# The low parts of the split weights move from VectorE to GpSimd, in a four-layer fp32 transformer kernel

## The chip, the cores and the metric

The kernel runs on one core of a Trainium2 chip. The metric is the device time of one execution in microseconds (us); lower is better. The time before is the median of three runs.

## The reference, cut to what matters

Two different transformer blocks run one after the other on the same residual (512 latent tokens, width 1024, plus 256 context tokens in the first block), each with two layers, so four layers in all. Every layer is: a modulated norm, a wide input projection, mixers (linear attention, neighbourhood and window attention in the first block; sparse attention and an mLSTM in the second), an output projection, a second modulated norm, and a gated feed-forward part. The weights stay fp32.

```python
h = rms_norm(x, g1) * (1 + scale) + shift
p = h @ w_in                       # 2848 columns in layers 1, 2; 3408 in layers 3, 4
y = mixers(p) @ w_out
x = x + gate * y                   # y is normed first in layers 3, 4
h = rms_norm(x, g2) * (1 + scale) + shift
y = (silu(h @ w_gate) * (h @ w_up)) @ w_down    # 2816 hidden columns
x = x + gate * y                   # y is normed first in layers 3, 4
```

## The kernel before, in words

TensorE takes its operands as fp32r, a rounded form. To keep accuracy each big product is made as three: high x high, high x low, low x high, where `high` is the rounded value and `low` is the value minus `high`, rounded again. This holds for the weights and for the activations (`h_high`, `h_low`, `hidden_high`, `hidden_low`).

The weights of a layer come as 108 split slices ("units"), 432 in the whole kernel, of up to 1024 columns on 128 partitions. Within a layer the order is fixed: 32 slices of the input projection (712 columns in layers 1 and 2, 852 in layers 3 and 4), 8 of the output projection, then three parts (`PARTS`) of the feed-forward. The first part has 16 gate and up slices and 8 down slices, the second and the third 14 and 8. Seven does not divide by two, so in each of those two parts the last slice of each half of the down projection has only 512 columns and half the matmuls. All other slices of the output projection and of the feed-forward have 1024.

Each slice goes through a chain of engines:

1. SyncE loads it into one of four landing slots (`weights`). Slot j is loaded again when `w_low` says that the low part of slice j - 4 has been made.
2. ScalarE makes the high part (`split()` of the scalar block, line 869): it waits for the load and for TensorE to be done with slice s - 2, since `weights_high` and `weights_low` are double buffers.
3. VectorE makes the low part (`split()` of the vector block, line 1197), waits for `w_high`, and increments `w_low`.
4. TensorE waits for `w_low` and uses the slice (line 461 in `product`, line 788 for gate and up).

Every engine works through its own queue in order, and the place of a `split()` in it is written out by hand. VectorE's stand: two before each `modulate` and before the `low` loop of the output projection, so behind what VectorE did last (a norm, the end of the mixers) and ahead of what TensorE waits for next; one for each slice beside the input projection; and in the feed-forward before and between the products of gate and up, and ahead of `outputs`, which empties the banks of the down projection. `modulate` (lines 1219 and 1209) reads a turned bank, scales it into `scratch` and subtracts `h_high` to give `h_low`; TensorE needs `h_low` for its first slices and for reusing the banks.

GpSimd does next to nothing before: two memsets in each of layers 1 and 2 (lines 839 and 841).

Of the kernel before, what the change touches and what calls it, by code (L numbers as in the profile page):

```python
# [22 lines left out]
F32 = mybir.dt.float32  # L23
F32R = mybir.dt.float32r
I32 = mybir.dt.int32
ALU = mybir.AluOpType
# [41 lines left out]
LAND = 4  # L68
# [94 lines left out]
def layer(nc, T, w, sems, second, with_ctx, nxt, start_loads=()):  # L163
# [5 lines left out]
    S = sems  # L169
# [29 lines left out]
    slots = [WR[:, UNIT * i:UNIT * (i + 1)] for i in range(LAND)]  # L199
    WH, WL = ([T[n][:, UNIT * i:UNIT * (i + 1)] for i in range(2)] for n in ("weights_high", "weights_low"))  # L200
# [30 lines left out]
    weight_units = []  # L231
    split_of = []
# [126 lines left out]
    if not second:  # L359
# [6 lines left out]
        ZT = SC[0:33, 12288:13056]  # L366
        WZ = SC[0:33, 13056:13568]
# [51 lines left out]
    with nc.Block() as block:  # L419
# [414 lines left out]

        @block.gpsimd
        def _(pool):
            if not second:
                pool.wait_ge(S["h_ready"], 1)
                pool.memset(WZ, 0.0).then_inc(S["zeroed"], 1)
                pool.wait_ge(S["zeroed"], 1)  # L840
                pool.memset(ZT[32:33, :], 1.0).then_inc(S["z_ones"], 1)

        @block.scalar
        def _(act):
# [301 lines left out]
        def _(dve):  # L1146
# [9 lines left out]
            def copy_out(bank, dst):  # L1156
                dve.tensor_copy(dst, bank).then_inc(S["emptied_dve"], 1)
# [28 lines left out]
                for i, t in list(enumerate(tt))[::2]:  # L1186
                    dve.tensor_scalar(XNV[:, t, :], XV[:, t, :], rstd[:, i:i + 1], None, ALU.mult).then_inc(S["normed%d" % which], 1)

            nsplit, nhigh = [0], [0]

            def split():

                s_ = nsplit[0]
                nsplit[0] += 1
                _, _, (k, n), _ = weight_units[split_of[s_]]
                dve.wait_ge(S["w_high"], s_ + 1)
                dve.tensor_tensor(WL[s_ % 2][:, 0:k * n], slots[split_of[s_] % LAND][:, 0:k * n],  # L1197
                                  WH[s_ % 2][:, 0:k * n].bitcast(F32), ALU.subtract).then_inc(S["w_low"], 1)

            def after_high():  # L1200

# [165 lines left out]
            dve.sem_inc(S["scales"], 1)  # L1367
            if start_loads:
                norm(0, IN_T)
            split()  # L1370
            split()
            modulate(0, IN_T)
            dve.wait_ge(S["emptied_dve"], B.emptied_by("d"))
            dve.sem_inc(S["h_ready"], 1)
# [46 lines left out]

            for j in range(8):
                for i in range(4 if j < 7 else 3):
                    if (j, i) != (0, 0):
                        split()
                    if second:
                        beside_projection(j, i)
                for i, t in enumerate(IN_T):
                    bank = B.empty(dve, turn[i % 2], "d")
                    if bank is not None:  # L1430
                        copy_out(bank[:, 0:CW], pr(t, CW * j, CW))

            if not second:
# [36 lines left out]
                for k in range(NCH - 1):  # L1470
                    for d in range(2):
                        c, after = order[d][k], order[d][k + 1]
                        i = c // 2
# [9 lines left out]
                for n, t in enumerate(OUT_T):  # L1483
# [17 lines left out]
                    if t >= CTX_T:  # L1501
                        i = t - CTX_T
# [11 lines left out]
                n = 0  # L1514
# [99 lines left out]
                dve.sem_inc(S["mixed"], 1)  # L1614


            split()
            split()
            for f in range(KD):
                for a, cnt, r in spans(OUT_T):  # L1620
                    low(f, a, cnt, after_high()[:, 0:cnt])
# [33 lines left out]
                        copy_out(bank[:, :], y)  # L1655

            for j in range(2):
                for _ in range(3):
                    split()
                outputs(0, j)  # L1660
            if second:
                add_normed(0)
            norm(1, OUT_T)
            dve.sem_inc(S["mod_room"], 1)
            split()
            split()
            modulate(1, OUT_T)


            def ahead():  # L1670
                if nsplit[0] < len(split_of):
                    split()

            q = 0
            for m0, m1 in PARTS:
                for m in range(m0, m1):
                    if m:
                        ahead()
                    for _ in spans(OUT_T):
                        B.empty(dve, "a", "d")  # L1680
                    gated = B.emptied_by("a") - len(spans(OUT_T))
                    ahead()
                    for a, cnt, r in spans(OUT_T):
                        dve.wait_ge(S["emptied_dve"], B.emptied_by("d"))
                        bank = B.empty(dve, "d", "d")
# [7 lines left out]
                    if nxt:  # L1693
                        mod_tile(m)
                for half in range(2):
                    for k in range(m0, m1, 2):
                        ahead()
                    outputs(1, half, more=m0 > 0)
                    if nxt and m1 == KF:
                        mod_tile(KF + half)  # L1700
# [167 lines left out]
```

## Time and profile before

| | |
|---|---|
| runs | 4343.82 us median (4338.45, 4343.82, 4361.6) |
| span of the profiled execution | 4364.2 us; its own time is not listed among the three runs |
| busy: TensorE, VectorE, ScalarE, GpSimd | 3728.4, 2047.7, 1124.4, 2.7 us |
| mean granted TensorE clock | 0.884 |
| low parts on VectorE | 432 instructions, 486.8 us |

The profile page lists, for one execution, each engine's busy time and what it waited for. The timeline lists instructions in order of time: start, length, engine, line of the kernel, operation, what it writes and reads, how many were merged, and in square brackets how long the engine sat idle before it and what it waited for. The window view gives busy time by engine in a stretch. Durations below come from this one execution, so a sum made of them belongs beside its span.

### The profile page before, as it was taken

What the parts mean: (1) busy time and instruction counts of PE and PEld (TensorE: products, weight loads), DVE (VectorE), ACT (ScalarE), POOL (GpSimd) and SP (SyncE); (2) the same over time, 40 slices, a digit from 0 to 9 for tenths busy, and PEclk for the clock granted to TensorE, in tenths of its full rate; (3) what the DMA queues carried; (4) which work ended last, traced back from release to release, by engine and by line L of the source; (5) the groups of instructions that cost most, each with busy time, mean ns of one, the idle gap of its engine ahead of it and who ended that gap; (6) DMA issues with size and microseconds to landing.
All of it is one profiled execution on the core that took longest, in us unless ns stands there. A gap on an engine that the chain in (4) does not pass through costs nothing. (4 is left out here: it accounts for less than half of the span.)

```text
span 4364.2 us, 51771 instructions
## 1 busy us (share of the span) xinstructions
PE 3728.4 (85%) x21178; PEld 3105.1 (71%) x21178; DVE 2047.7 (47%) x3763; ACT 1124.4 (26%) x1884; POOL 2.7 (0%) x8
## 2 busy tenths in 40 slices
PE   4896899899998995998999693878999793678997
PEld 3895667688887995777878682546888691456886
DVE  0324566423333325664443538664333448765333
ACT  0312344311111212443222321233222322323222
POOL 0000000000000000000000000000000000000000
PEclk9996699899999995899999895559999896769999
DMA  8110000232332210003445320003454230002332
GB/s 294 49 52 1 25 1 30 58 122 91 107 102 84 56 46 3 22 18 109 151 135 158 92 85 0 0 10 91 141 169 150 84 89 10 1 17 75 97 97 73
DMA packets 315485, 326.95 MB, mean 75 GB/s; under 512 B 11082, under 2 KB 231794, under 8 KB 315122
## 3 DMA queue, kind: packets, MB, share of 16 engines
q1 hardware_dynamic: 315250, 323.64, 24.4%
q8 instruction: 169, 2.77, 0.3%
q14 instruction: 66, 0.54, 0.0%
HBM read 321.50 MB, written 2.10 MB: 74 GB/s over the span
## 5 line engine op out<-in xcount | busy, mean ns | idle before, releaser
L1197 DVE TENSOR_TENSOR weights_low<-weights,weights_high 128x1024 fp32r<-128x1024 f32 (+3 forms) x432 | 486.8, 1129 | 1278.8 <-ACT weights_high L869 1276.9
L869 ACT ACTIVATE weights_high<-weights 128x1024 fp32r<-128x1024 f32 (+3 forms) x432 | 423.8, 983 | 1407.3 <-PE bank L461 997.4
L788 PE MATMUL bank<-h_high,weights_high 128*128 128x512 f32 (+1 forms) x1760 | 658.5, 374 | 10.4 <-DVE h_low L1209 9.1
L788 PE MATMUL bank<-h_low,weights_high 128*128 128x512 f32 (+1 forms) x1760 | 649.9, 369 | 0.0
L788 PE MATMUL bank<-h_high,weights_low 128*128 128x512 f32 (+1 forms) x1760 | 648.8, 369 | 0.0
L461 PE MATMUL bank<-weights_high,h_high 128*128 128x356 f32 (+2 forms) x1568 | 546.0, 348 | 6.4 <-DVE h_low L1209 6.0
L461 PE MATMUL bank<-weights_low,h_high 128*128 128x356 f32 (+2 forms) x1568 | 545.1, 348 | 0.0
L461 PE MATMUL bank<-weights_high,h_low 128*128 128x356 f32 (+2 forms) x1568 | 543.6, 347 | 0.0
L788 PEld LDWEIGHTS bank<-h_high,weights_high 128*128 128x128 f32 x1760 | 332.9, 189 | 83.5 <-DVE h_low L1209 16.5
L788 PEld LDWEIGHTS bank<-h_high,weights_low 128*128 128x128 f32 x1760 | 333.0, 189 | 55.8
L788 PEld LDWEIGHTS bank<-h_low,weights_high 128*128 128x128 f32 x1760 | 333.3, 189 | 52.2
L461 PEld LDWEIGHTS bank<-weights_high,h_high 128*128 128x128 f32 x1568 | 296.0, 189 | 22.4 <-issue 7.1
L461 PE MATMUL bank<-weights_high,hidden_high 128*128 128x512 f32 x792 | 309.9, 391 | 1.5 <-DVE weights_low L1197 1.4
L461 PE MATMUL bank<-weights_low,hidden_high 128*128 128x512 f32 x792 | 308.3, 389 | 0.0
L461 PEld LDWEIGHTS bank<-weights_high,h_low 128*128 128x128 f32 x1568 | 297.9, 190 | 14.4
L461 PE MATMUL bank<-weights_high,hidden_low 128*128 128x512 f32 x792 | 308.1, 389 | 0.0
L461 PEld LDWEIGHTS bank<-weights_low,h_high 128*128 128x128 f32 x1568 | 296.8, 189 | 13.5
L570 PEld LDWEIGHTS bank<-constants,scratch 128*128 128x128 f32 x792 | 100.0, 160 | 223.8 <-ACT scratch L935 125.0
L583 PE MATMUL bank<-projected,scratch 128*128 128x128 f32 x1584 | 253.7, 311 | 0.1
L583 PEld LDWEIGHTS bank<-projected,scratch 128*128 128x128 f32 x1584 | 236.6, 227 | 1.4 <-issue 1.0
L570 PE MATMUL bank<-constants,scratch 128*128 128x128 f32 x792 | 156.6, 324 | 89.1 <-ACT scratch L935 57.9
L557 PE MATMUL bank<-scratch 64*128 64x512 f32 (+3 forms) x320 | 165.6, 607 | 51.0 <-ACT scratch L1063 51.0
(232 smaller groups left out, 4165.3 us busy)
## 6 DMA issues: line engine op xcount, KB each, us to landing
projected<-in_w_mod SPq DMA_DIRECT2D x96, 1024.0 KB, 5.2
weights<-in_w_gate_up SPq DMA_DIRECT2D x88, 512.0 KB, 4.0
weights<-in_w_down SPq DMA_DIRECT2D x80, 512.0 KB, 3.9
weights<-in_w_in SPq DMA_DIRECT2D x64, 426.0 KB, 3.4
weights<-in_w_in SPq DMA_DIRECT2D x64, 356.0 KB, 3.1
weights<-in_w_gate SPq DMA_DIRECT2D x44, 512.0 KB, 6.6
weights<-in_w_up SPq DMA_DIRECT2D x44, 512.0 KB, 7.7
weights<-in_w_out SPq DMA_DIRECT2D x32, 512.0 KB, 3.6
```

Of the source, the lines that this page charges most:

```text
L461: mm = pe.matmul(out_banks[t][:, 0:n], x[:, kk - off[0], at], wt[:, kk - k, :], start=(kk == k0 and q == 0), stop=(kk == k1 - 1 and q == 2))
L557: mm = pe.matmul(b[:, 0:u["nb"]], u["q"], u["kb"], start=True, stop=True)
L570: mm = pe.transpose(PS[4 + j // 4][:, (j % 4) * PT:(j % 4 + 1) * PT], src[:, j * PT:(j + 1) * PT], ident)
L583: mm = pe.matmul(PS[6 + i % 2][:, 0:128], pb[:, j * PT:(j + 1) * PT], pr(t, c - u.get("off", 0), 128), start=(j == 0), stop=(j == len(u["v ...
L788: mm = pe.matmul(bank[:, 0:cnt], wt[:, k, :], x[:, k, a:a + cnt], start=(k == 0 and q == 0), stop=(k == KD - 1 and q == 2))
L869: act.activation(WH[s_ % 2][:, 0:k * n], slots[j % LAND][:, 0:k * n], ACT.Copy).then_inc(S["w_high"], 1)
L1197: dve.tensor_tensor(WL[s_ % 2][:, 0:k * n], slots[split_of[s_] % LAND][:, 0:k * n], WH[s_ % 2][:, 0:k * n].bitcast(F32), ALU.subtract).the ...
```

## The change: what it does

The 432 subtractions go to GpSimd's queue. Their operands, their number and the semaphores `w_high` and `w_low` are the same. All of VectorE's `split()` calls go. In layers 1 and 2 GpSimd's two memsets, which wait for VectorE's `h_ready`, stand before the third low part.

```diff
         @block.gpsimd
         def _(pool):
-            if not second:
-                pool.wait_ge(S["h_ready"], 1)
-                pool.memset(WZ, 0.0).then_inc(S["zeroed"], 1)
-                pool.wait_ge(S["zeroed"], 1)
-                pool.memset(ZT[32:33, :], 1.0).then_inc(S["z_ones"], 1)
+            for s_, j in enumerate(split_of):
+                _, _, (k, n), _ = weight_units[j]
+                if not second and s_ == 2:
+                    pool.wait_ge(S["h_ready"], 1)
+                    pool.memset(WZ, 0.0).then_inc(S["zeroed"], 1)
+                    pool.wait_ge(S["zeroed"], 1)
+                    pool.memset(ZT[32:33, :], 1.0).then_inc(S["z_ones"], 1)
+                    pool.wait_ge(S["z_ones"], 1)
+                pool.wait_ge(S["w_high"], s_ + 1)
+                pool.tensor_tensor(WL[s_ % 2][:, 0:k * n], slots[j % LAND][:, 0:k * n],
+                                   WH[s_ % 2][:, 0:k * n].bitcast(F32), ALU.subtract).then_inc(S["w_low"], 1)
...
-            def split():
-
-                s_ = nsplit[0]
-                nsplit[0] += 1
-                _, _, (k, n), _ = weight_units[split_of[s_]]
-                dve.wait_ge(S["w_high"], s_ + 1)
-                dve.tensor_tensor(WL[s_ % 2][:, 0:k * n], slots[split_of[s_] % LAND][:, 0:k * n],
-                                  WH[s_ % 2][:, 0:k * n].bitcast(F32), ALU.subtract).then_inc(S["w_low"], 1)
...
                 norm(0, IN_T)
-            split()
-            split()
             modulate(0, IN_T)
...
             for j in range(2):
-                for _ in range(3):
-                    split()
                 outputs(0, j)
...
             dve.sem_inc(S["mod_room"], 1)
-            split()
-            split()
             modulate(1, OUT_T)
...
                 for half in range(2):
-                    for k in range(m0, m1, 2):
-                        ahead()
                     outputs(1, half, more=m0 > 0)
```

The other calls of `split()` and `ahead()` in the vector block (beside the input projection, before the `low` loop of the output projection, and around the products of gate and up) go in the same way.

## Rows read from the trace of the kernel before

**Rows 1.** The page, part 1: busy us, share of the span, instructions.
```profile
PE 3728.4 (85%) x21178; PEld 3105.1 (71%) x21178; DVE 2047.7 (47%) x3763; ACT 1124.4 (26%) x1884; POOL 2.7 (0%) x8
```

**Rows 2.** Windows: length, busy us of each engine (instructions), clock, DMA share, GB/s.
```profile
811.00:1390.00 579.00, 575.99 (x3626) 490.70 (x3627) 199.75 (x295) 90.06 (x114) 0.00 (x0) 0.99 0.32 99
...
3978.00:4342.00 364.00, 360.94 (x1587) 296.61 (x1585) 143.24 (x168) 84.08 (x95) 0.00 (x0) 1.00 0.29 87
```

**Rows 3.** Groups of VectorE instructions by shape: busy us, mean ns, idle before.
```profile
L1197 DVE TENSOR_TENSOR weights_low<-weights,weights_high 128x1024 fp32r<-128x1024 f32 x288 | 351.4, 1222 | 830.0 <-ACT weights_high L869 829.0
...
L1691 DVE TENSOR_TENSOR hidden_low<-projected,hidden_high 128x512 fp32r<-128x512 f32 x88 | 60.9, 692 | 3.0
...
L1197 DVE TENSOR_TENSOR weights_low<-weights,weights_high 128x712 fp32r<-128x712 f32 x64 | 57.5, 901 | 233.1 <-ACT weights_high L869 232.9
```

**Rows 4.** Waits of TensorE: us in total, times, longest us.
```profile
PE bank L461 <- DVE weights_low L1197: 1.9, 3, 1.2
```

**Rows 5.** Timeline, feed-forward of layer 4, ScalarE and VectorE.
```profile
4031.56 1.05 ACT L869 ACTIVATE weights_high<-weights 128x1024 fp32r<-128x1024 f32 x1
...
4036.56 1.06 ACT L869 ACTIVATE weights_high<-weights 128x1024 fp32r<-128x1024 f32 x1 [3.95 <-PE bank L788]
...
4032.64 1.23 DVE L1197 TENSOR_TENSOR weights_low<-weights,weights_high 128x1024 fp32r<-128x1024 f32 x1 [3.82 <-ACT weights_high L869]
```

**Rows 6.** Timeline, input projection of layer 3, VectorE and ScalarE.
```profile
2517.70 1.05 DVE L1197 TENSOR_TENSOR weights_low<-weights,weights_high 128x852 fp32r<-128x852 f32 x1 [3.62 <-ACT weights_high L869]
...
2521.42 0.92 ACT L869 ACTIVATE weights_high<-weights 128x852 fp32r<-128x852 f32 x1 [0.70 <-PE bank L461]
```

**Rows 7.** Timeline, down projection of layer 2, around a slice of 512 columns.
```profile
2252.17 1.06 ACT L869 ACTIVATE weights_high<-weights 128x1024 fp32r<-128x1024 f32 x1 [4.81 <-PE bank L461]
...
2253.26 1.23 DVE L1197 TENSOR_TENSOR weights_low<-weights,weights_high 128x1024 fp32r<-128x1024 f32 x1 [5.18 <-ACT weights_high L869]
...
2254.55 0.19 PEld L461 LDWEIGHTS bank<-weights_high,hidden_high 128*128 128x128 f32 x1 [0.17 <-DVE weights_low L1197]
...
2260.20 2.50 DVE L1197 TENSOR_TENSOR weights_low<-weights,weights_high 128x1024 fp32r<-128x1024 f32 x2
...
2261.48 0.50 PE L461 MATMUL bank<-weights_high,hidden_high 128*128 128x512 f32 x1 [1.19 <-DVE weights_low L1197]
```

**Rows 8.** Timeline of GpSimd.
```profile
148.50 0.52 POOL L839 MEMSET scratch<- 33x512 f32 x1 [148.05 <-DVEq L1374]
149.08 0.73 POOL L841 MEMSET scratch<- 1x768 f32 x1
```

**Rows 9.** Timeline, end of the mixers of layer 3.
```profile
2929.92 1.99 ACT L869 ACTIVATE weights_high<-weights 128x1024 fp32r<-128x1024 f32 x2
...
2930.33 2.29 DVE L1239 TENSOR_TENSOR projected<-projected,small 128x2048 f32<-128x2048 f32 x1
...
2934.98 2.29 DVE L1243 TENSOR_TENSOR projected<-projected 128x2048 f32<-128x2048 f32 x1
2937.41 5.84 PEld L759 LDWEIGHTS bank<-constants,projected 128*128 128x128 f32 x32 [13.26 <-issue]
```

**Rows 10.** Timeline, second norm of layer 3, VectorE and ScalarE.
```profile
2989.71 1.28 DVE L1639 SCALAR_TENSOR_TENSOR projected<-projected,small,gates 128x1024 f32<-128x1024 f32 x1
...
3005.91 0.81 DVE L1219 TENSOR_SCALAR scratch<-bank,small 128x512 f32<-128x512 f32 x1 [0.56 <-PE bank L480]
...
2989.37 1.99 ACT L869 ACTIVATE weights_high<-weights 128x1024 fp32r<-128x1024 f32 x2
```

**Rows 11.** Timeline, first modulation of layer 1.
```profile
127.77 1.71 DVE L1197 TENSOR_TENSOR weights_low<-weights,weights_high 128x712 fp32r<-128x712 f32 x2 [1.81 <-ACT weights_high L869]
...
129.97 0.42 DVE L1209 TENSOR_TENSOR h_low<-scratch,h_high 128x256 fp32r<-128x256 f32 x1
```

**Rows 12.** Timeline, start of the output projection of layer 1.
```profile
714.06 2.36 DVE L1197 TENSOR_TENSOR weights_low<-weights,weights_high 128x1024 fp32r<-128x1024 f32 x2
...
714.52 6.97 ACT L1094 ACTIVATE h_high<-bank 128x256 fp32r<-128x256 f32 x16 [1.89 <-PE bank L759]
...
716.34 5.99 DVE L1209 TENSOR_TENSOR h_low<-bank,h_high 128x256 fp32r<-128x256 f32 x13
```

More of the change, by code:

```diff
@@ L1187, in norm @@
                     dve.tensor_scalar(XNV[:, t, :], XV[:, t, :], rstd[:, i:i + 1], None, ALU.mult).then_inc(S["normed%d" % which], 1)
-            nsplit, nhigh = [0], [0]
-            def split():
-                s_ = nsplit[0]
-                nsplit[0] += 1
-                _, _, (k, n), _ = weight_units[split_of[s_]]
-                dve.wait_ge(S["w_high"], s_ + 1)
-                dve.tensor_tensor(WL[s_ % 2][:, 0:k * n], slots[split_of[s_] % LAND][:, 0:k * n],
-                                  WH[s_ % 2][:, 0:k * n].bitcast(F32), ALU.subtract).then_inc(S["w_low"], 1)
+            nhigh = [0]
             def after_high():
@@ L1423, in _ @@
                 for i in range(4 if j < 7 else 3):
-                    if (j, i) != (0, 0):
-                        split()
                     if second:
@@ L1657, in _ @@
             for j in range(2):
-                for _ in range(3):
-                    split()
                 outputs(0, j)
@@ L1664, in _ @@
             dve.sem_inc(S["mod_room"], 1)
-            split()
-            split()
             modulate(1, OUT_T)
-            def ahead():
-                if nsplit[0] < len(split_of):
-                    split()
             q = 0
@@ L1676, in _ @@
                 for m in range(m0, m1):
-                    if m:
-                        ahead()
                     for _ in spans(OUT_T):
@@ L1681, in _ @@
                     gated = B.emptied_by("a") - len(spans(OUT_T))
-                    ahead()
                     for a, cnt, r in spans(OUT_T):
@@ L1695, in _ @@
                 for half in range(2):
-                    for k in range(m0, m1, 2):
-                        ahead()
                     outputs(1, half, more=m0 > 0)
```

## The prediction

> **What bounds the kernel now.** I read the page first: TensorE is busy for 85% of the span and VectorE for 47% [rows 1], so nothing that merely relieves VectorE pays on average. The window view then splits the span. In the stretches of weight products TensorE is busy without a break: 575.99 of 579 us in the first feed-forward, 360.94 of 364 in the last [rows 2]; thirteen such windows hold 2868 us, with TensorE busy for 2822. Only the list of waits says what the low parts cost there, and it is almost nothing: 1.9 us in 3 waits [rows 4], one more of 1.2 us on the feed-forward line, and 13.3 us of weight loads held back, mostly the same places. The rest of the time lies between products, in norms, mixers and modulations, where VectorE and TensorE take turns. So the change can act in three places: in the chain of a slice beside the products, at the slices with no slack, and where a low part stands in or beside a VectorE chain on which TensorE waits.
>
> **What one low part costs on GpSimd.** The trace before has no such instruction. On VectorE 1024 columns take 1222 ns [rows 3], and that is the lower end. GpSimd's only rows are memsets: 512 columns in 0.52 us and 768 in 0.73 [rows 8], so 0.82 ns for each column written, and some 0.1 us besides. If the two reads pass in turn, 1024 columns take 0.1 + 2 x 0.84 = 1.8 us; if the write takes its turn too, 0.1 + 3 x 0.84 = 2.6. I take the middle, 2.2 us, 1.0 more than VectorE; 1.85 for 852 columns, 1.55 for 712, 1.2 for 512. All 432 come to some 870 us, a fifth of the span, so GpSimd is not full.
>
> The Trainium skill, GPSIMD Engine Reference, section 3.1, gives 4497 ns for a two-input fp32 instruction of 2048 columns; half of that, as an estimate, is 2.25 us, and the sum would be the same.
>
> **Beside the products: nothing.** In layer 4, ScalarE's high part starts at 4031.56, VectorE's low part ends at 4033.87, and TensorE closes the slice before at 4036.56, when the next high part starts [rows 5]. TensorE runs on about 0.2 us before that, so 2.4 us are spare, and 1.0 is used. In the input projection of layers 3 and 4 the low part ends at 2518.75 and the next high part starts at 2521.42 [rows 6]: again 2.4 spare, of which 0.8 is used. Layers 1 and 2 have 3.8 there. I went through all 432 slices in this way, comparing the end of the low part with the first matmul of its slice. Half the gate and up slices have less, 2.04, but there the low part stood 0.86 to 1.06 us behind VectorE's own work, which GpSimd doesn't do, so they lose next to nothing. SyncE's loads wait for `w_low` too and start 1 us later, but three slices (over 14 us) ahead of use. The two memsets, 1.3 us with their waits, now delay the third low part of layers 1 and 2, with 3.8 us spare. What covers all this is the 4.7 us and more that TensorE needs for a slice; the cover ends at a low part of about 3.6 us.
>
> **Slices after a short one: +6.9.** A slice of 512 columns keeps TensorE only 2.9 us in layers 2 to 4. The next slice's high part runs 2252.17 to 2253.23, its low part to 2254.49, and TensorE loads it at 2254.55 [rows 7]: 0.14 us spare by the matmuls. There are seven such places (two in layers 2 and 3, three in layer 4), and one in layer 2 where the load was late (0.06 spare). 8 x (1.0 - 0.14) = +6.9 us.
>
> **Where VectorE's queue held the low part back: -3.0.** In layer 2 two slices waited 4.25 us for VectorE, busy emptying banks, and TensorE stalled 1.19 us [rows 7], then 1.20, and 0.22 at a third; layer 3 has one of 0.44. GpSimd has no such queue: -3.0.
>
> **Output projection, layers 1 and 2: -2.6.** VectorE makes two low parts from 714.06 and reaches `h_low` at 716.34, while ScalarE has the first `h_high` by about 714.95 [rows 12]. Here the subtraction reads a bank, and TensorE's turning waits for emptied banks. It starts 1.3 us earlier, twice. In layers 3 and 4 the turning takes TensorE 5.84 us without waiting [rows 9], so there is nothing to gain. At the second modulation VectorE waits for a bank anyway (0.56 us, [rows 10]): also nothing.
>
> **VectorE chains that share time with GpSimd's new work: the term that decides.** The rows say which instructions will overlap, not whether they delay each other. If they can't run together, the second waits for all of the first, and only instructions with both inputs in SBUF count.
> - End of the mixers, layers 3 and 4. The high parts are ready at about 2930.95 and 2931.91, in the midst of three dependent VectorE instructions of 2.29 us from 2930.33 to 2937.27, after which TensorE, idle for 13.26 us, starts [rows 9]. VectorE waits on a semaphore between them, so GpSimd's low parts slip in: 2 x 2.2 = 4.4, in two layers +8.8.
> - Second norm, layers 3 and 4. The high parts come at about 2990.4 and 2991.36, and VectorE has eight dependent instructions from 2989.71 [rows 10]: again +4.4 in each, +8.8.
> - First modulation. In layers 1 and 2 two low parts would hold GpSimd until 127.8 + 3.1 = 130.9; `h_low` started at 129.97 [rows 11]: +0.9 each. In layers 3 and 4 from 2440.8 to 2444.5, against 2443.54: +1.0 each. Together +3.8.
>
> These are +21.4 if they exclude each other, and if not about -2 (the modulations start up to 0.5 us earlier). Which end? Rows before can't say, since GpSimd never ran beside VectorE. I take the upper end, because each low part needs the same reads that VectorE's instruction does and gives them back only when it ends.
>
> The Trainium skill, SBUF — State Buffer, section on the single rule, says that a VectorE instruction with two SBUF inputs contends with a GpSimd instruction that reads SBUF, and that the second to issue blocks until the first is done. No row here shows it. By that rule the sum is what I forecast; without it the sum is that of the first rival.
>
> **Sum.** +6.9 - 3.0 - 2.6 + 21.4 = +22.7 us on the profiled span of 4364.2, which makes 4386.9, or 0.52%. The span is 20 us above the median of the runs, and I add the same microseconds to the median: 4343.8 + 22.7 = 4366.
>
> **The rivals.**
> - No exclusion: GpSimd and VectorE run side by side. Sum +6.9 - 3.0 - 2.6 - 2 = -0.7: 4343 us, not slower. For it: the two engines have queues of their own, and nothing in the rows ties them. Against it: only the two-input argument. It decides by the lengths of the three 2.29 us instructions: unchanged, it holds.
> - GpSimd becomes the bound. If a low part takes over 3.6 us, every second gate and up slice stalls. At 4.5 us (twice my price): 4.5 - 1.22 - 2.4 = 0.9 us on about 130 slices of layers 2 to 4, plus 8 x 3.1 and four chains of two low parts, 9 each: +180, about 4520. Against it: it is far above the 2.6 us that three streams give.
> - The relief is worth more: VectorE's queue gets 487 us free. If all twelve stage starts moved by the two low parts that stood there (2.36 us at 1024 columns), -25 in all, with +6.9 for the short slices and -3.0: 4322. Against it: VectorE was idle at two kinds of start after them [rows 10], and TensorE turned without waiting [rows 9].
>
> **How the numbers follow.** Chances: exclusion (full or in part) 0.70, no exclusion 0.17, GpSimd as the bound 0.08, larger relief 0.05. The prediction is the first, 4366. With prices from 1.8 to 2.6 its sum runs from about +15 to +32, and with only some low parts landing in the chains it falls to about +5: its own range is 4349 to 4378. The range of 8 in 10 takes in the no-exclusion rival and some drift of the median (the three runs spread over 23 us): 4338 to 4388. A difference of 0.5% (21.7 us) is about what a measurement tells from none. The exclusion case ends above it about half the time: 0.36, and the bound case adds 0.08, so slower 0.44; faster 0.05; within it 0.51.
>
> **What would show it.** Right: low parts of about 2.2 us on GpSimd; the three instructions at the end of the mixers stretching from 6.9 to about 11.4 us in layers 3 and 4; TensorE waits for GpSimd of some 0.9 us after the short slices; the product windows otherwise unchanged; the 1.19 us stall gone. Wrong: two-input instructions of VectorE at their old lengths beside GpSimd (first rival), or TensorE waits for `weights_low` all along the feed-forward (second). The prediction fails most easily on the order at each boundary: if VectorE keeps its turn, both chains stay whole.

## The result and the profile after

| | before | after |
|---|---|---|
| median of 20 runs each, same chip | 4358.60 us (4325.03 to 4373.29) | 4390.73 us (4361.19 to 4416.52) |
| ratio, 95% interval | | 1.0078 (1.0056 to 1.0101) |
| span of the profiled execution | 4364.2 us | 4388.9 us |
| its mean granted TensorE clock | 0.884 | 0.874 |

The change makes the kernel slower, by 0.8%. The prediction was 4366 us, with 8 chances in 10 for 4338 to 4388; the median lies 2.7 us above that range. Two later timings of the same kernel, six runs each, gave 1.0100 (1.0059 to 1.0142) and 1.0103 (1.0062 to 1.0143).

The page after, part 1, answers to [rows 1]:

```profile
PE 3727.8 (85%) x21178; PEld 3105.0 (71%) x21178; DVE 1844.9 (42%) x3331; ACT 1124.0 (26%) x1884; POOL 968.2 (22%) x440
```

VectorE lost 486.8 us of work, but its busy time fell by only 202.8. The missing 284 us are the first sign: VectorE's other instructions became longer. The groups of instructions by shape say which (busy us, mean ns, idle before):

```profile
L846 POOL TENSOR_TENSOR weights_low<-weights,weights_high 128x1024 fp32r<-128x1024 f32 x288 | 704.4, 2447 | 2642.2 <-ACT weights_high L875 2642.2
L846 POOL TENSOR_TENSOR weights_low<-weights,weights_high 128x852 fp32r<-128x852 f32 x64 | 130.5, 2040 | 258.0 <-ACT weights_high L875 258.0
...
L1671 DVE TENSOR_TENSOR hidden_low<-projected,hidden_high 128x512 fp32r<-128x512 f32 x88 | 232.9, 2646 | 3.0
L1620 DVE TENSOR_TENSOR x_res<-x_res,projected 128x512 f32<-128x512 f32 x80 | 97.1, 1214 | 2.7
L1669 DVE TENSOR_TENSOR projected<-projected,bank 128x512 f32<-128x512 f32 x88 | 60.6, 688 | 596.7 <-PE bank L788 596.7
L1670 DVE TENSOR_TENSOR hidden_high<-projected,bank 128x512 fp32r<-128x512 f32 x88 | 59.8, 680 | 0.0
```

`hidden_low`, with both inputs in SBUF, took 692 ns before [rows 3] and takes 2646. Its two neighbours, which read a bank, stay at 0.69 us. A low part costs GpSimd 2.40 us when nothing disturbs it (2.45 on average), against 1.22 on VectorE [rows 3].

The timeline shows how the two engines exclude each other. First in the feed-forward of layer 4, which answers to [rows 5]:

```profile
4058.31 0.68 DVE L1670 TENSOR_TENSOR hidden_high<-projected,bank 128x512 fp32r<-128x512 f32 x1
4059.02 2.77 DVE L1671 TENSOR_TENSOR hidden_low<-projected,hidden_high 128x512 fp32r<-128x512 f32 x1
...
4058.85 2.40 POOL L846 TENSOR_TENSOR weights_low<-weights,weights_high 128x1024 fp32r<-128x1024 f32 x1 [2.62 <-ACT weights_high L875]
```

GpSimd reads from 4058.85 to 4061.25. `hidden_low` is issued at 4059.02 and ends at 4061.79, 0.54 us after GpSimd: it did nothing until GpSimd was done, and the profile counts its wait as busy time. It costs nothing, since VectorE's next instruction, at 4068.59, waits 6.79 us for TensorE anyway.

Then the down projection of layer 2, after a slice of 512 columns, which answers to [rows 7]:

```profile
2249.56 0.69 DVE L1618 TENSOR_TENSOR projected<-bank,gates 128x512 f32<-128x512 f32 x1 [16.75 <-PE bank L461]
2250.29 2.65 DVE L1620 TENSOR_TENSOR x_res<-x_res,projected 128x512 f32<-128x512 f32 x1
2252.97 0.69 DVE L1618 TENSOR_TENSOR projected<-bank,gates 128x512 f32<-128x512 f32 x1
2253.69 2.05 DVE L1620 TENSOR_TENSOR x_res<-x_res,projected 128x512 f32<-128x512 f32 x1
...
2250.01 2.37 POOL L846 TENSOR_TENSOR weights_low<-weights,weights_high 128x1024 fp32r<-128x1024 f32 x1 [4.58 <-ACT weights_high L875]
2252.73 2.47 POOL L846 TENSOR_TENSOR weights_low<-weights,weights_high 128x1024 fp32r<-128x1024 f32 x1 [0.34 <-ACT weights_high L875]
...
2252.44 0.50 PE L461 MATMUL bank<-weights_high,hidden_high 128*128 128x512 f32 x1 [0.94 <-POOL weights_low L846]
```

At 2252.97 an instruction that reads a bank and one SBUF operand runs wholly beside GpSimd (2252.73 to 2255.20) in its 0.69 us; the next, with two SBUF operands, ends at 2255.74, again 0.54 us after GpSimd. TensorE waits 0.94 us for the low part: the short slice. Its list of waits for GpSimd, which answers to [rows 4], has nine entries. Seven are the short slices; the other two, 0.64 and 0.80 us in layer 2, follow slices whose load was late (ScalarE had waited 2.88 and 3.05 us for it):

```profile
PE bank L461 <- POOL weights_low L846: 4.4, 5, 1.0
...
PE bank L788 <- POOL weights_low L846: 3.7, 4, 1.0
```

The windows of the first and the last feed-forward answer to [rows 2]:

```profile
813.10:1392.10 579.00, 575.23 (x3628) 490.50 (x3628) 183.84 (x230) 89.03 (x113) 156.24 (x66) 0.99 0.33 99
4003.00:4367.00 364.00, 358.38 (x1572) 294.57 (x1572) 107.41 (x97) 81.15 (x93) 154.04 (x66) 1.00 0.29 87
```

In the first window TensorE is as busy as before (575.23 of 579, 575.99 before), though GpSimd now has 156 us of low parts there. In the last it loses 2.6 us, most of it at three short slices.

The start of the output projection of layer 1 answers to [rows 12]:

```profile
713.95 4.67 POOL L846 TENSOR_TENSOR weights_low<-weights,weights_high 128x1024 fp32r<-128x1024 f32 x2 [393.01 <-ACT weights_high L875]
...
716.71 3.61 ACT L1100 ACTIVATE h_high<-bank 128x256 fp32r<-128x256 f32 x9 [1.89 <-PE bank L759]
717.20 0.42 DVE L1206 TENSOR_TENSOR h_low<-bank,h_high 128x256 fp32r<-128x256 f32 x1 [1.09 <-PE bank L759]
```

The first `h_low` now starts 0.49 us after the first `h_high`, not 1.82, and beside GpSimd's low part (to 718.62) it keeps its 0.42 us, as it reads a bank.

The end of the mixers of layer 3 answers to [rows 9]:

```profile
2925.71 2.29 DVE L1236 TENSOR_TENSOR projected<-projected,small 128x2048 f32<-128x2048 f32 x1
2926.41 8.13 POOL L846 TENSOR_TENSOR weights_low<-weights,weights_high 128x1024 fp32r<-128x1024 f32 x2 [338.92 <-ACT weights_high L875]
2928.03 4.31 DVE L1237 TENSOR_TENSOR projected<-projected 128x2048 f32<-128x2048 f32 x1
...
2932.38 4.31 DVE L1240 TENSOR_TENSOR projected<-projected 128x2048 f32<-128x2048 f32 x1
2936.82 5.45 PEld L759 LDWEIGHTS bank<-constants,projected 128*128 128x128 f32 x32 [17.29 <-issue]
```

The engines alternate at the boundaries between instructions. GpSimd is issued at 2926.41 but waits for VectorE's first instruction, which ends at 2928.00; then each of the next two VectorE instructions is 2.02 us longer, as it waits for a low part. The three take 10.98 us instead of 6.94 [rows 9], and TensorE is idle for 17.29 us instead of 13.26.

The second norm of layer 3 answers to [rows 10]:

```profile
2989.50 5.99 POOL L846 TENSOR_TENSOR weights_low<-weights,weights_high 128x1024 fp32r<-128x1024 f32 x2 [10.70 <-ACT weights_high L875]
2990.04 3.25 DVE L1631 TENSOR_TENSOR x_res<-x_res,projected 128x1024 f32<-128x1024 f32 x1
2993.21 3.36 DVE L1630 SCALAR_TENSOR_TENSOR projected<-projected,small,gates 128x1024 f32<-128x1024 f32 x1
...
2997.75 1.28 DVE L1630 SCALAR_TENSOR_TENSOR projected<-projected,small,gates 128x1024 f32<-128x1024 f32 x1
```

Two of VectorE's eight instructions grow, by 2.02 and 2.08 us. The first modulation of layer 1 answers to [rows 11]:

```profile
129.49 3.36 POOL L846 TENSOR_TENSOR weights_low<-weights,weights_high 128x712 fp32r<-128x712 f32 x2 [129.04 <-ACT weights_high L875]
...
131.65 1.48 DVE L1206 TENSOR_TENSOR h_low<-scratch,h_high 128x256 fp32r<-128x256 f32 x1
```

The first `h_low` ends at 133.13, 0.28 us after GpSimd.

The Trainium skill, SBUF — State Buffer, section Who interferes with whom, says that a VectorE instruction with two SBUF inputs contends with a GpSimd instruction that reads SBUF, and that the one that issues second blocks until the first is done. The trace agrees: the waiting instruction ends 0.54 us after GpSimd's in the feed-forward of layer 4 and in the down projection of layer 2, though it was issued 2.23 us before GpSimd's end at one place and 1.51 at the other.

### Where the microseconds went

I cut both executions at the same matmuls by their number, and took the difference of each stretch, from the first matmul on. Outside the mixers the change adds 23.2 us:

| term of the prediction | forecast | measured |
|---|---|---|
| slices after a short one, with VectorE's queue | +6.9 - 3.0 = +3.9 | +5.1 (layers 1 to 4: -0.15, +0.90, +1.42, +2.92) |
| start of the output projection, up to the first product | -2.6 | -3.0 (-1.01, -0.21, -0.39, -1.38) |
| first modulations | +3.8 | +4.2 (+1.05, +1.03, +1.08, +1.08) |
| end of the mixers, layers 3 and 4 | +8.8 | +7.9 (+4.03, +3.89) |
| second norm and turning, layers 3 and 4 | +8.8 | +10.0 (+5.25, +4.74) |
| all else outside the mixers (+2.3 of it ahead of the first modulation, where no low part had been made) | 0 | -1.0 |
| sum | +22.7 | +23.2 |

Two rows agree better than their reasons do. The forecast of the output projection was -1.3 us in each of layers 1 and 2 and nothing in layers 3 and 4. Layer 1 gave -1.0; in layer 2 the turning ran without a stop before and after (3.68 and 3.69 us), and only 0.2 was gained. The other -1.8 came from layers 3 and 4, where the 32 matmuls of the turning took 5.66 and 5.20 us at a granted clock of 0.64 and 0.70, against 6.05 and 6.58 at 0.60 and 0.55. The kernel before, run again, shows -0.6 and -0.3 at the same two places, and the kernel with nothing but two delays in each of layers 3 and 4 (below) -0.1 and -1.4. So over half of that row is luck. The second norm is taken up at the end.

The mixers themselves differ by +2.1 us in all, made of terms as large as -4.5 and +9.3, and there is not one low part inside them. The windows of the mixers of layers 3 and 4 show what goes with their length (length; busy us of TensorE, its weight loads, VectorE, ScalarE, GpSimd; granted clock; DMA share; GB/s). Before:

```profile
2596.73:2924.02 327.29, 210.87 (x683) 136.96 (x684) 221.02 (x555) 81.44 (x174) 0.00 (x0) 0.58 0.01 4
3594.81:3892.33 297.52, 175.59 (x684) 112.98 (x684) 219.89 (x555) 81.42 (x174) 0.00 (x0) 0.68 0.01 4
```

After:

```profile
2594.45:2919.41 324.96, 207.64 (x684) 134.03 (x684) 220.72 (x555) 81.41 (x174) 0.00 (x0) 0.60 0.01 4
3600.16:3906.94 306.78, 186.36 (x684) 120.54 (x684) 220.32 (x555) 81.41 (x174) 0.00 (x0) 0.66 0.01 4
```

The same 684 matmuls keep TensorE busy for 176 us at a granted clock of 0.68 and for 211 at 0.58. VectorE's work is the same in all four rows to 1.2 us. Keep this in mind for the experiments.

### The profile page after: what moved, and what is told of

Read it like the earlier page. It is cut to its first block and busy times, and to the rows that moved or that the text cites. A ratio compares the mean times of both kernels' runs of the same rounds, so it can differ in the third digit from the quotient of the medians.

```text
span 4388.9 us, 51755 instructions
## 1 busy us (share of the span) xinstructions
PE 3727.8 (85%) x21178; PEld 3105.0 (71%) x21178; DVE 1844.9 (42%) x3331; ACT 1124.0 (26%) x1884; POOL 968.2 (22%) x440
## 5 line engine op out<-in xcount | busy, mean ns | idle before, releaser
L846 POOL TENSOR_TENSOR weights_low<-weights,weights_high 128x1024 fp32r<-128x1024 f32 (+3 forms) x432 | 965.5, 2236 | 3354.6 <-ACT weights_high L875 3354.5
L1669 DVE TENSOR_TENSOR projected<-projected,bank 128x512 f32<-128x512 f32 (+1 forms) x110 | 69.8, 635 | 775.8 <-PE bank L788 775.8
L1163 DVE COPY projected<-bank 128x356 f32<-128x356 f32 (+2 forms) x112 | 66.7, 596 | 667.4 <-PE bank L461 667.4
L1671 DVE TENSOR_TENSOR hidden_low<-projected,hidden_high 128x512 fp32r<-128x512 f32 (+1 forms) x110 | 245.6, 2233 | 3.8
```

The costliest lines, as they stand in the source:

```text
L846: pool.tensor_tensor(WL[s_ % 2][:, 0:k * n], slots[j % LAND][:, 0:k * n], WH[s_ % 2][:, 0:k * n].bitcast(F32), ALU.subtract).then_inc(S["w ...
L1669: dve.tensor_tensor(FT[:, 0:cnt], SG[q % 2][:, 0:cnt], bank[:, 0:cnt], ALU.mult)
L1671: dve.tensor_tensor(GL[:, m - m0, at], FT[:, 0:cnt], GH[:, m - m0, at].bitcast(F32), ALU.subtract).then_inc(S["emptied_dve"], 1)
```

## The experiments

All times are compared with runs of the kernel before on the same chip. "Outside the mixers" is the difference of the stretches from the profiled execution of before, summed as above; I call it the profile sum, and it needs no timing. Most kernels share this edit, with another `on_vector` in each; VectorE's `split()` calls are back, and skip what GpSimd makes:

```diff
+def on_vector(second, s_):        # second: layers 3 and 4; s_: number of the slice
+    return s_ in (...)
...
+                if on_vector(second, s_):
+                    continue
+                if s_ and on_vector(second, s_ - 1):
+                    pool.wait_ge(S["w_low"], s_)
                 pool.wait_ge(S["w_high"], s_ + 1)
                 pool.tensor_tensor(...)
```

**Theory and rival.** Theory: the engines exclude each other, and three kinds of place pay for it (the first modulations, the end of the mixers, the second norm); the short slices pay for GpSimd's longer instruction. Rival: the time comes from anything GpSimd does all along (its load, its queue, TensorE's clock), and the places are only part of it.

### GpSimd waits until the chains are done

```diff
+                if second and s_ == 32:
+                    pool.wait_ge(S["mixed"], 1)
+                if second and s_ == 40:
+                    pool.wait_ge(S["mod_room"], 1)
```

> GpSimd makes all low parts, but in layers 3 and 4 the two of the output projection wait until VectorE's chain at the end of the mixers is done, and the two of the first gate and up slices until its second norm is done. Exclusion theory: the four stretches of about 4.0 us each go, two modulations get some 1 us longer each; of the changed kernel's +24 us on the profile about +10 stay (ratio 1.002). Rival, that GpSimd's longer instruction itself is what TensorE waits for at these places: the starts get later still, since GpSimd begins later, and the ratio stays at 1.008 or rises.

Measured: 1.003 (0.9997 to 1.0063). Outside the mixers +10.6. In the end of the mixers of layer 3 all three instructions are back at 2.29 us:

```profile
2912.67 2.29 DVE L1262 TENSOR_TENSOR projected<-projected,small 128x2048 f32<-128x2048 f32 x1
2914.99 2.29 DVE L1263 TENSOR_TENSOR projected<-projected 128x2048 f32<-128x2048 f32 x1
2917.32 2.29 DVE L1266 TENSOR_TENSOR projected<-projected 128x2048 f32<-128x2048 f32 x1
```

The same low parts on the same engine, a few us later, cost this chain nothing. At the second norm of layers 3 and 4, 2.3 and 2.2 us stay. In all, 12.6 of the 23.2 us are gone, so they were the overlap in time.

### VectorE keeps the slices of the stage starts, of the short places, or both

```diff
     return s_ in (0, 1, 32, 33, 40, 41)                # stage starts
     return s_ in (82, 86, 104)                         # after a short slice
     return s_ in (0, 1, 32, 33, 40, 41, 82, 86, 104)   # both
```

> VectorE keeps the six low parts at the starts of the three products of each layer (numbers 0, 1, 32, 33, 40, 41), GpSimd makes the other 102. Exclusion theory: mixers' end, second norm and modulations as in the kernel before; the gain at the output projection of layers 1 and 2 (1.0 us there) goes too; what stays is the short slices, +7, and the stalls removed in layer 2, -3: about +4 us, ratio 1.001. Rival, that the 10 us between the profiles' difference (+24.7) and the measured one (+34) comes from TensorE's clock in the mixers, which anything on GpSimd or a longer program brings about: 1.003 or more.

> VectorE keeps only the low parts that follow the short slices (numbers 82, 86, 104), GpSimd makes all others. By the price of a low part alone (2.4 us against 1.2): seven stalls of about 1.1 us go, so about 7 us less than the changed kernel, +17 us on the profile, ratio 1.005 to 1.006. If VectorE's queue makes them late instead, TensorE still waits there and the ratio stays near 1.008.

> VectorE keeps the starts and the ones after the short slices, nine in each layer, GpSimd makes the other 99. Exclusion and price together: both losses gone, the stalls in layer 2 still removed: -3 us on the profile, ratio 0.999 to 1.000. Rival, that GpSimd beside VectorE in the feed-forward costs something by itself (the product of gate and up waits three times as long for its last step): the ratio stays at 1.002 or more.

Measured, in this order: 1.0029 (0.9995 to 1.0063), 1.0061 (1.0025 to 1.0096), and 0.999 (0.9959 to 1.0021); both together once more on another chip, 1.0038 (1.0005 to 1.007). Outside the mixers: -1.7, +15.2, and -4.7 (-3.2 the second time).

> VectorE keeps the nine low parts of each layer at the starts and after the short slices, as in the experiment before. Outside the mixers -4 to -5 us, as measured. If GpSimd's work in the other 99 slices lowers TensorE's clock in the mixers, the timed ratio lies at 1.001 to 1.003, some 10 us above that; if not, at 0.999.

So the stage starts are worth 23.2 + 1.7 = 24.9 us of the profile and the short places 23.2 - 15.2 = 8.0, each to within the few us by which an unchanged kernel moves (below). In the feed-forwards of layers 2 to 4 alone, the change stands 2.1, 2.6 and 3.8 us above the kernel that keeps the short places on VectorE, 8.5 us for seven places: 1.2 us each. The expectations of +17 with the short places on VectorE and of -3 with all nine came about as written. With the stage starts on VectorE +4 was expected and -1.7 came: the four feed-forwards alone stand at +4.5, and the rest is spread over stretches in which unchanged kernels differ as much. The timings lie above the profile sums: the stage starts left to VectorE still gave +13 us (0.29%, an interval that just includes none) with -1.7, and the nine places +4 us and then +18 in the mean with -4.7 and -3.2.

### The chains alone

The kernel before, with only slices 32, 33, 40 and 41 of layers 3 and 4 on GpSimd, 8 low parts of 432:

```diff
     return not (second and s_ in (32, 33, 40, 41))
```

> The kernel before, with only four low parts of layers 3 and 4 on GpSimd: the two made while VectorE works through the end of the mixers and the two made during its second norm; VectorE makes the other 424. Exclusion theory: +4.0 us at each of these four places and, as they no longer stand ahead of the modulation, nothing gained: about +16 us on the profile, ratio 1.0035 to 1.004. Rival, that only GpSimd's whole load slows the kernel: no change, ratio 1.000.

Measured: 1.0056 (1.0027 to 1.0085). Outside the mixers +13.0, where +16 was expected; 4.04, 5.31, 4.01 and 4.78 of it stand at the four places, and -5.1 in all the rest. The same rows of the end of the mixers come back:

```profile
2929.36 2.29 DVE L1258 TENSOR_TENSOR projected<-projected,small 128x2048 f32<-128x2048 f32 x1
2931.68 4.31 DVE L1259 TENSOR_TENSOR projected<-projected 128x2048 f32<-128x2048 f32 x1
2936.03 4.31 DVE L1262 TENSOR_TENSOR projected<-projected 128x2048 f32<-128x2048 f32 x1
```

Eight low parts bring over half of the profile's loss. That speaks against the rival, that it is GpSimd's whole load.

### GpSimd reads once instead of twice

```diff
-                pool.tensor_tensor(WL[s_ % 2][:, 0:k * n], slots[j % LAND][:, 0:k * n],
-                                   WH[s_ % 2][:, 0:k * n].bitcast(F32), ALU.subtract).then_inc(S["w_low"], 1)
+                pool.tensor_copy(WL[s_ % 2][:, 0:k * n], slots[j % LAND][:, 0:k * n]).then_inc(S["w_low"], 1)
```

This leaves out the subtraction.

> The changed kernel, but GpSimd only copies the landed slice into weights_low instead of subtracting the high part, so one input in place of two (the low parts are wrong by that). If what excludes VectorE is any read of SBUF by GpSimd: VectorE's two-input instructions still stretch, by GpSimd's shorter time of 1.0 to 1.3 us each, and the four chains of layers 3 and 4 get 2 to 2.5 us longer in place of 4. If it is GpSimd's second input that excludes VectorE: VectorE's instructions keep their old lengths of 0.69 and 2.29 us. If a copy costs GpSimd as much as the subtraction: 2.4 us and the same stretches.

One execution: 4330.95 us, beside a median of 4357.86 for before. The groups by shape:

```profile
L855 POOL CAST weights_low<-weights 128x1024 fp32r<-128x1024 f32 x288 | 314.0, 1091 | 2974.2 <-ACT weights_high L883 2974.2
...
L1709 DVE TENSOR_TENSOR hidden_low<-projected,hidden_high 128x512 fp32r<-128x512 f32 x88 | 119.7, 1360 | 3.0
```

And the end of the mixers of layer 3:

```profile
2884.13 2.29 DVE L1257 TENSOR_TENSOR projected<-projected,small 128x2048 f32<-128x2048 f32 x1
2886.45 3.01 DVE L1258 TENSOR_TENSOR projected<-projected 128x2048 f32<-128x2048 f32 x1
2889.50 3.00 DVE L1261 TENSOR_TENSOR projected<-projected 128x2048 f32<-128x2048 f32 x1
```

With one input GpSimd takes 1.09 us instead of 2.45, and VectorE is still held, by that much less: `hidden_low` takes 1360 ns instead of 2646, and the chain stretches by 1.43 us instead of 4.04. So one read is enough to exclude, and the price follows the length of GpSimd's instruction. Outside the mixers the sum is -8.3.

### GpSimd works without reading

The kernel before, with nine memsets of a spare tile of 80 columns on GpSimd after each high part. The second kernel has one memset of one column instead:

```diff
...
+            done = 0
+            for s_ in range(len(split_of)):
+                pool.wait_ge(S["w_high"], s_ + 1)
+                for _ in range(9):
+                    done += 1
+                    pool.memset(T["spare"], 0.0).then_inc(S["pool_step"], 1)
+                    pool.wait_ge(S["pool_step"], done)
```

> The kernel before, VectorE making all low parts, and after each high part GpSimd writes zeros nine times into a spare tile of 80 columns, each after the one before: some 2 us for each slice, reading nothing. If only reads exclude: VectorE's two-input instructions keep their lengths, nothing outside the mixers moves, ratio 1.000. If writes exclude too, VectorE's chains in layers 3 and 4 stretch. If a busy GpSimd lowers TensorE's clock in the mixers: +10 to +15 us there, ratio 1.002 to 1.004.

> The kernel before, and after each high part GpSimd writes one column of zeros (0.1 us) and goes back to waiting. If it is enough that GpSimd is in the loop of the slices: +10 to +15 us in the mixers, ratio 1.002 to 1.004. If only its load matters, or nothing of it: 1.000.

Measured: 0.9998 (0.9971 to 1.0025) and 0.9979 (0.9955 to 1.0002). Outside the mixers -3.9 and -1.3. In the first of them:

```profile
L848 POOL MEMSET spare<- 128x80 f32 x3888 | 640.5, 165 | 3468.1 <-ACT weights_high L877 3267.9 <-POOL spare L848 0.5
...
L1699 DVE TENSOR_TENSOR hidden_low<-projected,hidden_high 128x512 fp32r<-128x512 f32 x88 | 60.9, 692 | 3.0
```

640 us of GpSimd work at the same moments, and `hidden_low` stands at its old 692 ns, to the nanosecond. GpSimd's load alone costs nothing: this rival falls. The subtraction and the copy exclude, the memset does not, and what the first two have and the third lacks is a read of SBUF.

### The kernels against themselves

> The kernel before, unchanged. If the 10 us by which the timed runs of the changed kernel exceed the difference of the profiles are chance in TensorE's granted clock during the mixers, this one lies off 1.000 by up to 0.3% too, and its profile differs from that of before by tens of us in the mixers of layers 3 and 4 alone. If the clock is steady for one and the same program, it lies at 1.000 within 0.1%.

> The kernel before, unchanged, a second time. If the kernels with GpSimd in them are truly about 13 us slower than their profiles outside the mixers say, this one stays within 0.2% of 1.000, as the first did (0.9985).

> The changed kernel again. Outside the mixers its profile should lie at +23 us as before; the timed ratio, if the rest is chance, anywhere from 1.003 to 1.009, and if something systematic adds 10 us, again at 1.008.

> The changed kernel once more, for the 10 us still open. Outside the mixers +23 us again. If chance in the granted clock makes the rest, its runs together with the 26 before come nearer to +23 us; if something systematic does, they stay at +30 or more.

The kernel before against itself: 0.9985 (0.9956 to 1.0013) and 1.0004 (0.9983 to 1.0024), profile sums -3.8 and -2.9. The mixers of layers 3 and 4 in the first of these two:

```profile
2594.78:2901.72 306.94, 186.43 (x683) 120.52 (x684) 220.42 (x555) 81.42 (x174) 0.00 (x0) 0.66 0.01 4
3570.22:3865.93 295.71, 174.99 (x684) 112.44 (x684) 219.92 (x555) 81.42 (x174) 0.00 (x0) 0.68 0.01 4
```

The same program has layer 3's mixers in 306.9 us at a clock of 0.66 here and in 327.3 at 0.58 in the profile of before: 20 us that no instruction explains. Three readings follow. Profile sums of a few us outside the mixers are noise too: an identical program gives -3 to -4. The profile of before, from which all sums are taken, is itself a long one: the two repeats and the two kernels with memsets stand at -3.8, -2.9, -3.9 and -1.3, so beside the mean of the five the change's three profiles are about +25 and the nine places on VectorE -1 to -2. And one execution's span says little of a change of this size.

The change again gave 1.01 (1.0059 to 1.0142) and 1.0103 (1.0062 to 1.0143), with profile sums +22.7 and +21.9.

### Later starts without GpSimd

The timings of the change lie above its profile sums. The 32 runs of it have a mean of 4393 us, the 115 runs of before 4357.5 (95% interval +-2.9, one run of 7231.85 left out): +36, where the profile has +23. To see whether lateness alone does that, VectorE makes 20 copies of four columns, 4.05 us, at the end of the mixers and ahead of the second norm in layers 3 and 4 of the kernel before:

```diff
+                for _ in range(20):
+                    step(dve.tensor_copy(rr, fl))
```

> The kernel before without GpSimd in it, but VectorE makes twenty small dependent copies, about 4 us in all, at the end of the mixers and ahead of the second norm of layers 3 and 4, where the exclusion cost 4 us each. Outside the mixers +16 us. If later starts alone, by their place in time, bring TensorE to a lower clock in the mixers: another 10 to 15 us, ratio 1.006 to 1.007; if it takes GpSimd: 1.0035 to 1.004.

Measured: 1.0069 (1.0044 to 1.0095), a mean of +28 us. Outside the mixers only +11.7 (4.08, 3.94, 2.99 and 2.32 at the four places, -1.6 in all the rest). The expectation of +16 outside the mixers was missed, since the second norm grew by only 2.3 to 3.0; the ratio of 1.006 to 1.007 that was expected if later starts alone matter came true. The mean granted clock of its 12 runs is 0.8762, that of before 0.8815 over 115 runs, that of the change 0.878 in its 20. So with nothing added on GpSimd, 12 us of delay came out as 28.

### A version that might beat both

VectorE keeps the stage starts of layers 3 and 4, the first modulations, and the short places. GpSimd keeps the starts of the output projection and second modulation in layers 1 and 2, where its low parts come earlier:

```diff
     return s_ in (0, 1, 82, 86, 104) or second and s_ in (32, 33, 40, 41)
```

> As the one with nine low parts on VectorE, but in layers 1 and 2 GpSimd also makes the four ahead of the output projection and of the gate and up product, where nothing collides with a chain on the path: 1.2 us less than it at the start of the output projections, so -6 us outside the mixers, ratio 0.998 to 0.999 if nothing lowers the clock.

Measured: 1.0039 (1.0007 to 1.0071), with a profile sum of -6.6. It is no faster; by the timing it is slower, against the 0.998 to 0.999 that was expected. Neither this version nor the one that keeps all nine gives a gain that can be measured.

The profiles hold a pattern in the mixers of layer 4. In five of them VectorE makes all low parts and nothing is delayed (before, its two repeats, the nine memsets and the single one): 297.5, 295.7, 297.5, 297.5 and 310.3 us, in this order. In the twelve others the same stretch takes 306.8 to 328.9, with the nine places on VectorE too:

```profile
3591.55:3920.42 328.87, 213.64 (x684) 137.69 (x684) 221.06 (x555) 81.46 (x174) 0.00 (x0) 0.58 0.01 4
```

This row is from the first run of that version. The repeated kernel before entered the same mixers at 3591.68 and took 297.49 us at 0.68. So the mixers of layer 4 get longer in the changed kernels though no low part stands in them, and here without a later start. In layer 3 there is no such split: 306.9 to 327.3 in the five, 292.7 to 328.9 in the twelve. These are single executions, and no run here shows the cause.

## Why the prediction was right and wrong

- **The mechanism was right.** Exclusion (0.70) holds. VectorE instructions with two SBUF inputs wait for the whole of GpSimd's, those with a bank operand don't, and the order at the boundaries lets both low parts in.
- **The price of a low part** was 2.2 us taken, 2.40 measured; 852 columns 2.04 against 1.85. The Trainium skill, GPSIMD Engine Reference, section 3.1, by the same halving gives an estimate of 2.25; the trace has 2.40.
- **End of the mixers:** right in place and order. VectorE is held 2.02 us for each low part, not 2.2. The three instructions took 10.98 us where 11.4 was expected.
- **Second norm:** the chain grew by 4.1 of the 4.4 forecast. The rest of the +5.25 of layer 3, a term that the prediction did not have, is TensorE's turning behind it: 6.39 us for 32 matmuls instead of 5.26. The granted clock was 0.69 in that window before and, after,

```profile
3007.00:3013.40 6.40, 6.37 (x33) 6.40 (x34) 4.25 (x7) 4.86 (x7) 0.00 (x0) 0.56 1.01 309
```

  0.56, near the lower of the two levels (1.2 of 2.4 GHz). TensorE had idled for 20.98 us ahead of it, 16.86 before. But one repeat of the unchanged kernel has the long turning after the short wait; its row, and that of before:

```profile
2980.87 6.65 PE L480 MATMUL bank<-constants,projected 128*128 128x128 f32 x32 [16.86 <-DVE projected L1187]
...
3003.90 5.26 PE L480 MATMUL bank<-constants,projected 128*128 128x128 f32 x32 [16.86 <-DVE projected L1187]
```

  In all profiles, the ten turnings after 20.98 us of waiting (layers 3 and 4 of five kernels) took 6.15 to 6.56 us; of the eighteen after 16.86, sixteen took 5.16 to 5.53 and two 6.60 and 6.65. After 19.57, in the kernel with delays, it took 5.54 and 5.15. So the turning was long at every wait of 21 us, but a wait a few us longer than before does not by itself make it long.
- **Short slices:** seven places were right. The eighth hung on a late load, and which loads are late changes from one execution to the next: the two such waits of layer 2 (0.64 and 0.80 us) are missing from one of the change's three profiles. The size was too small: 1.2 us each, not 0.86. The low part costs 0.2 us more than taken, and the first matmul after the stall takes 0.50 us instead of 0.41.
- **VectorE's queue:** right. Two stalls of layer 2 went, 1.5 us each from matmul to matmul, and 0.5 at the third.
- **Output projection:** mostly luck, as said above: -1.2 of the -2.6 in layers 1 and 2, and -1.8 in layers 3 and 4, where nothing was forecast.
- **Beside the products:** nothing, right, but for 0.64 and 0.80 us after two late loads of layer 2. With the seven short slices these are all the waits of TensorE for GpSimd.
- **No exclusion, GpSimd as the bound, larger relief:** all three fell, the first by `hidden_low` at 2646 ns, the second by a low part of 2.45 us where 3.6 was needed, the third by -3.0 us at the output projections and +4.2 at the first modulations, where -25 in all was needed.

**What was wrong** is the last step: "I add the same microseconds to the median: 4343.8 + 22.7 = 4366." It failed twice.

First, the base. The median of three runs was 4343.8; that of twenty on the same chip is 4358.6, and the mean of 115 is 4357.5. This is 15 of the 25 us by which the median missed the forecast. With this base alone put right, the forecast is 4381 and its range 4353 to 4403, which holds the 4390.7 measured. The prediction saw that the profiled span stood 20 us above the median and took the median's side. The range allowed for "some drift of the median", too little: the twenty runs of the kernel before spread over 48 us. (The upper end of the prediction's own range, 4378, is 34 us above the base where the sum behind it gives 32; nothing hangs on it.)

Second, the sum of a profile is not the difference of the timings. The profile's +23.2 (+25 beside the mean of the five profiles) became +32 in the medians (+36 in the means of all runs). Shown: the mixers of one program run 20 us longer in one execution than in another, at the clock that they are granted (306.9 and 327.3 above), and a kernel with two delays and nothing on GpSimd has such a surplus too (28 timed, 12 in the profile). Weighed by the mean granted clock of each run (a fit within each kernel over all 292 runs gives 17 us for each 0.01), the change's first 20 runs stand at +25 (+-6) instead of +31, close to the profile, and the kernel with the delays at +19 (+-7) instead of +28. So a good part of the surplus goes with TensorE's granted clock. Such a fit does not say what lowered the clock.

Open: what lowers the grant, and how much of the surplus is chance. Later stage starts can't be all of it: the versions that keep the nine slices on VectorE, with a profile sum of -4 and no later start, have a mean of +11 over 24 runs, and the last version +16 with -6.6 at a mean clock of 0.8754. Those with memsets as the added work on GpSimd have -0.5 and -7. Twelve runs of an unchanged program gave -5 and +7, so half of such a surplus can be chance. That the mixers of layer 4 were longer in all twelve profiles of changed kernels than in four of the five others speaks against chance alone. Whether this comes from the moved instants of the matmuls, or from GpSimd's reading, no run here separates.

## What to carry to other kernels

Before moving work to GpSimd, list what VectorE does with two SBUF inputs at the same moments, and ask who waits for it: beside a full TensorE such a wait was free here, and in a chain on which TensorE waits each GpSimd instruction of 2.40 us cost 2.0, so hold it back by a semaphore there. VectorE's busy time is no measure of the relief, since the time that it is blocked counts as busy. Forecast against as many runs of the base as there are, and where a stage with sparse matmuls runs at a varying clock, give the range at least the spread of that stage.

## What the runs showed of the hardware

- VectorE instructions with two operands in SBUF and GpSimd instructions that read exclude each other as wholes (2.29 us became 4.31). GpSimd's read of one operand is enough (VectorE's 0.69 us became 1.36 beside a 1.09 us copy); 3888 memsets, which read nothing, changed nothing.
- The profile counts the blocked time as busy time: 486.8 us of work left VectorE, and its busy time fell by 202.8.
- VectorE instructions with one operand in a bank run beside GpSimd at full speed: 0.69 us at 2252.97.
- GpSimd took 2.40 us for a subtraction of 1024 fp32 columns, with two operands, and 1.09 for a copy that rounds them, with one.
- In the mixers of layer 3 the granted clock of the same program was 0.58 in one execution and 0.66 in another, and the stage 327.3 and 306.9 us long.
